# One layer of a hybrid decoder on one core: projecting the values of all heads ahead of the heads

## The reference

```
h = rms_norm(x, norm1_g)                      # x: 1024 tokens x 1024
proj = h @ w_in                               # columns: q 512, k 512, v 512, pool 512, gates 2048
q, k = rms_norm(q), rms_norm(k)               # 4 heads x 2 components x 64
a = (softmax(q1 k1^T / 8) - lam * softmax(q2 k2^T / 8)) v     # causal, v: 128 per head
a = rms_norm(a) * (1 - lam_init)
merged = sigmoid(gate0) * (a @ w_up_attn) + sigmoid(gate1) * (pool_mixer(xp) @ w_up_pool)
x = x + merged @ w_o
x = x + square(relu(rms_norm(x) @ w_mlp_in)) @ w_mlp_out
```

## Time and profile before

| | |
|---|---|
| median of three runs | 1267.37 us (1267.27 to 1267.81) |
| the profiled execution itself | 1267.24 us |
| its span in the profile | 1265.3 us (1.9 us lie around it) |
| PE busy | 98% of the span |
| DVE, ACT, POOL busy | 76%, 44%, 13% |
| granted clock, mean | 1.0 |
| chain that ended last | PE 90%, DVE 5% |

### The profile page before, as it was taken

One profiled execution on the slowest core, in us unless ns is written; L12 is line 12 of the kernel. 1 busy time (PEld: TensorE's weight loads), 2 busy tenths in 40 slices (PEclk: granted clock), 3 DMA queues, 4 the chain that ended last, 5 costly groups with the idle time before them and its releaser, 6 DMA issues.

```text
span 1265.3 us, 17523 instructions
## 1 busy us (share of the span) xinstructions
PE 1241.7 (98%) x6057; PEld 1043.6 (82%) x6057; DVE 960.4 (76%) x1442; ACT 560.9 (44%) x981; POOL 163.8 (13%) x293
## 2 busy tenths in 40 slices
PE   5999999999999999999999999999999999999998
PEld 5888888887888888888887888888888888888887
DVE  5877776768987769774588777777778898879764
ACT  5656555656553323322345455355454433333330
POOL 2433423333100040000000000000000000000034
PEclk9999999999999999999999999999999999999999
DMA  8010010100545466432214544534559644362323
GB/s 264 24 51 18 15 52 1 50 17 17 175 150 191 143 221 215 161 106 93 89 62 141 175 139 144 175 136 148 175 202 355 241 166 167 100 233 100 100 100 133
DMA packets 111816, 165.97 MB, mean 131 GB/s; under 512 B 5357, under 2 KB 59266, under 8 KB 111746
## 3 DMA queue, kind: packets, MB, share of 16 engines
q1 hardware_dynamic: 111746, 165.05, 38.3%
HBM read 116.80 MB, written 48.23 MB: 130 GB/s over the span
## 4 chain that ended last, share of the span: by engine, by line
PE 90%; DVE 5%; issue 2%; ACT 2%; DMA 1%; POOL 0%; SPq 0%; DVEq 0%; ACTq 0%; POOLq 0%
PE bank L2152 83%; PE bank L2331 3%; PE bank L2256 2%; PE bank L2207 1%; DVE c L2061 1%; DVE pair_lo L1955 1%; DMA raw<-in_w_in 1%; PE bank L2461 1%; PE bank L2314 1%; ACT slot_hi L925 0%; DVE wT_lo L1476 0%; DVE slot_lo L1376 0%; DVE small L1469 0%; DVE featT_lo L1391 0%; PE bank L2169 0%
## 5 line engine op out<-in xcount | busy, mean ns | idle before, releaser
L2152 PE MATMUL bank<-o_hi,s_hi 128*128 128x512 f32 x448 | 174.4, 389 | 0.0
L2152 PE MATMUL bank<-o_hi,s_lo 128*128 128x512 f32 x448 | 174.3, 389 | 0.0
L2152 PE MATMUL bank<-slot_hi,featT_hi 128*128 128x384 f32 (+1 forms) x320 | 118.1, 369 | 4.9 <-DVE slot_lo L1376 3.1
L2152 PE MATMUL bank<-slot_lo,featT_hi 128*128 128x384 f32 (+1 forms) x320 | 111.9, 350 | 0.0
L2152 PE MATMUL bank<-slot_hi,featT_lo 128*128 128x384 f32 (+1 forms) x320 | 111.6, 349 | 0.0
L2061 DVE TENSOR_TENSOR c<-bank,c 128x512 f32<-128x512 f32 x112 | 75.7, 689 | 35.0 <-PE bank L2152 33.3
L2152 PE MATMUL bank<-featT_hi,pair_hi 128*128 128x512 f32 x256 | 99.9, 390 | 0.8 <-DVE c L2061 0.6
L2152 PE MATMUL bank<-featT_lo,pair_hi 128*128 128x512 f32 x256 | 99.6, 389 | 0.0
L2152 PE MATMUL bank<-featT_hi,pair_lo 128*128 128x512 f32 x256 | 99.6, 389 | 0.0
L2152 PE MATMUL bank<-o_lo,s_hi 128*128 128x512 f32 x256 | 99.6, 389 | 0.0
L2152 PEld LDWEIGHTS bank<-o_hi,s_hi 128*128 128x128 f32 x448 | 84.1, 188 | 17.7 <-DVE s_lo L2005 0.4
(11 more groups left out here) (250 smaller groups left out, 3159.0 us busy)
## 6 DMA issues: line engine op xcount, KB each, us to landing
s_raw<-u_store SPq DMA_DIRECT2D x28, 1024.0 KB, 5.6
pair_raw<-in_w_mlp_in SPq DMA_DIRECT2D x16, 1024.0 KB, 5.9
u_store<-s_tile SPq DMA_DIRECT2D x64, 256.0 KB, 2.1
o_raw<-in_w_mlp_out SPq DMA_DIRECT2D x16, 1024.0 KB, 7.8
u_store<-u_tile SPq DMA_DIRECT2D x48, 256.0 KB, 2.4
gate_store<-out_tile SPq DMA_DIRECT2D x32, 256.0 KB, 2.1
gate_raw<-in_w_in SPq DMA_DIRECT2D x8, 1024.0 KB, 5.5
raw<-in_w_in SPq DMA_DIRECT2D x15, 512.0 KB, 4.7
```

The lines of the kernel that those rows point to most:

```text
L2152: mm = nc.tensor.matmul(out, a, b, start=start and i == 0, stop=stop and i == len(steps) - 1)
```

## The change

A new stage stands between the start and head 0. SP loads the value columns of w_in for all four heads (load_v_w, four loads of 512 KB with two blocks of features each), ACT and DVE split them into v_w, which lies where qT, kT, v_tok and wT lie later. PE then runs v_project for token tiles 0 to 7, each 24 matmuls of 512 columns into PSUM bank 4 or 5, with x_transpose(t + 1) ahead of v_project(t). ACT and DVE split the result into v_part (two buffers), and SP stores it to DRAM (v_store), 512 KB per tile. The treatment of x is done in this stage; x_transpose and its ACT, DVE and POOL parts leave head 0.

The heads then project q and k only: project is 24 matmuls of 256 columns, qkv is 256 wide, and POOL's split_v is gone. The values of a head are read back to v_tok in one load of 1 MB (load_v): for head 0 after all stores, for heads 1 to 3 when PE has done all products with v of the head before (out_full at T * h). PE waits for it (v_in) ahead of the first product with v of the head. One weight slot less is split between heads. The first exponential waits for all stores of v_part, whose place prob takes.

On ACT the order at the start is now x_square(0), v_w_hi(0), v_w_hi(1), x_hi(0), v_w_hi(2), v_w_hi(3), x_square(1), x_square(2); on DVE x_norm(0), v_w_lo(0), v_w_lo(1), x_lo(0), x_norm(1), v_w_lo(2), v_w_lo(3).

```diff
+        v_w = both("v_w", 96, [P, KD, HEADS * P], 16)
+        v_part = [at(f"v_part{i}", 144 + 4 * i, [P, HEADS, 2, P], F32R) for i in range(2)]
...
-        qkv = [at(f"qkv{i}", kb, [P, 3 * P]) for i, kb in enumerate((156, 157.5, 221))]
+        qkv = [at(f"qkv{i}", kb, [P, 2 * P]) for i, kb in enumerate((156, 157.5, 221))]
...
+        v_store = nc.dram_tensor("v_store", [HEADS, P, T, 2, P], F32, kind="Internal").ap()
...
-            return 2 * b + (t != 1)
+            return 2 * (t % 2) + b
...
+        def v_bank(t):
+
+            return PROJ + t % 2
+
+        def head_w(h, i):
+
+            return HEADS + 3 * h + 1 + i
...
+            def load_x(t):
+
+                wait(sp, h_ready, t - 3)
+                sp.dma_start(x_tile[t % 4][:], x_rows[t]).then_inc(x_in[t % 4], 16)
+
+            def load_v_w(i):
+
+                src = w_in_v[:, 2 * i:2 * i + 2, V0:V0 + HEADS * P]
+                sp.dma_start(k4(raw[i][:], 2), src).then_inc(raw_in[i], 16)
+
+            def load(r, src, left):
+
+                sp.wait_ge(w_ready, left)
+                if not isinstance(left, int):
...
-                dst, n = k4(raw[r][:], parts), parts // pieces
-                for i in range(pieces):
-                    sp.dma_start(dst[:, n * i:n * i + n], src[:, n * i:n * i + n]).then_inc(raw_in[r], 16)
+                sp.dma_start(k4(raw[r][:], KD), src).then_inc(raw_in[r], 16)
...
             def load_head(h):
-                for i, c0 in enumerate((0, K0, V0)):
-                    load(i, w_in_v[:, :, bass.ds(c0 + h * P, P)], 4 * h + 1 + i, pieces=PIECES[i])
-                load(3, w_in_v[:, :, bass.ds(X0 + (GROUPS - 1 - h) * P, P)], 4 * h + 4)
-
-            sp.dma_start(x_tile[0][:], x_rows[0]).then_inc(x_in[0], 16)
-            for i, c0 in enumerate((0, K0, V0)):
-                load(i, w_in_v[:, :, c0:c0 + P], 1 + i, pieces=PIECES[i])
-                if i == 0:
-                    sp.dma_start(g1_row[:], norm1_g.to_broadcast([P, D])).then_inc(g1_in, 16)
-            sp.dma_start(x_tile[1][:], x_rows[1]).then_inc(x_in[1], 16)
-            sp.dma_start(x_tile[2][:], x_rows[2]).then_inc(x_in[2], 16)
+                first = isinstance(h, int)
+                for i, c0 in enumerate((0, K0)):
+                    load(i, w_in_v[:, :, bass.ds(c0 + h * P, P)], 1 + i if first else head_w(h, i) - 3)
+                load(3, w_in_v[:, :, bass.ds(X0 + (GROUPS - 1 - h) * P, P)], 4 if first else head_w(h, 2) - 3)
+
+            def load_v(h):
+
+                if isinstance(h, int):
+                    sp.wait_ge(v_full, T)
+                    sp.wait_ge(v_out, 16 * T)
+                    src = v_store[h:h + 1]
+                else:
+                    sp.wait_ge(out_full, T * h)
+                    apart(sp)
+                    src = v_store[bass.ds(h, 1)]
+                sp.dma_start(v_tok[:].bitcast(F32), src.rearrange("o p t a c -> (o p) t a c")).then_inc(v_in, 16)
+
+            load_x(0)
+            load_v_w(0)
+            sp.dma_start(g1_row[:], norm1_g.to_broadcast([P, D])).then_inc(g1_in, 16)
+            load_v_w(1)
+            load_x(1)
+            load_v_w(2)
+            load_v_w(3)
+            load_x(2)
...
+            def store_v(t):
+
+                sp.wait_ge(v_ready, t + 1)
+                wait(sp, v_out, 16 * t)
+                sp.dma_start(v_store[:, :, t].rearrange("h p a c -> p h a c"), v_part[t % 2][:].bitcast(F32)).then_inc(v_out, 16)
+
+            load_x(3)
+            load_x(4)
+            load_x(5)
+            load_head(0)
+            for t in range(T):
+                if t + 6 < T:
+                    load_x(t + 6)
+                store_v(t)
+            load_v(0)
             with sp.Fori(1, HEADS) as h:
                 load_head(h)
...
 
             def gate_cols(n, width):
                 return w_in_v[:, :, G0 + n * P:G0 + n * P + width]
...
-            def split_v(h, s):
...
-                if not there:
-                    return
-                if t == 0:
-                    wait(pool, out_full, T * of)
-                pool.wait_ge(proj_free, use_of(of, t))
-                apart(pool)
-                v = qkv[t % 3][:, 2 * P:3 * P]
-                pool.tensor_copy(v_tok[:, t, 0, :], v).then_inc(v_hi, 1)
-                pool.wait_ge(v_hi, u + 1)
-                pool.tensor_tensor(v_tok[:, t, 1, :], v, v_tok[:, t, 0, :], ALU.subtract).then_inc(v_ready, 1)
...
-            for t in range(3):
+
+            for t in range(T):
                 x_inverse(t, x_squared, x_mean, x_inv)
...
-                    wait(act, v_ready, u - 1 if t < 2 else u - 2)
-                    nc.scalar.activation(qkv[t % 3][:], bank[:, PROJ, 0:3 * P], ACT.Copy).then_inc(proj_free, 1)
+                    nc.scalar.activation(qkv[t % 3][:], bank[:, PROJ, 0:2 * P], ACT.Copy).then_inc(proj_free, 1)
...
+                if isinstance(u, int) and u == 0:
+                    act.wait_ge(v_out, 16 * T)
...
-                        for i in range(3):
+                        for i in range(2):
                             head_weights(h, i)
...
+            def v_w_hi(i):
+
+                act.wait_ge(raw_in[i], 16)
+                nc.scalar.activation(v_w[0][:, 2 * i:2 * i + 2, :], k4(raw[i][:], 2), ACT.Copy).then_inc(w_hi, 1)
+
+            def v_hi_part(t):
+
+                act.wait_ge(v_full, t + 1)
+                wait(act, v_out, 16 * (t - 1))
+                nc.scalar.activation(v_part[t % 2][:, :, 0, :], k4(bank[:, v_bank(t), :], HEADS), ACT.Copy).then_inc(v_hi, 1)
+
             x_square(0)
-            for i in range(3):
-                split_hi(1 + i, i, PIECES[i], slots[i])
-                if i == 1:
-                    x_hi(0)
+            v_w_hi(0)
+            v_w_hi(1)
+            x_hi(0)
+            v_w_hi(2)
+            v_w_hi(3)
             x_square(1)
             x_square(2)
+            for t in range(T):
+                if t + 1 < T:
+                    x_hi(t + 1)
+                if t + 3 < T:
+                    x_square(t + 3)
+                v_hi_part(t)
+                if t == 4:
+                    act.wait_ge(lam_step, 2)
+                    nc.scalar.activation(lam_exp, lam_sum, ACT.Exp).then_inc(lam_exped, 1)
+                if t == 5:
+                    split_hi(head_w(0, 0), 0, 2, slots[0])
...
-                    if s == 0 and not first:
-                        head_weights(h - 1, 2)
...
+            dve.wait_ge(const_ready, 2)
             for i in range(16):
                 nc.vector.memset(count_inv[:, i:i + 1], 1.0 / (i + 1))
+            def v_w_lo(i):
+
+                dve.wait_ge(w_hi, i + 1)
+                cut = (slice(None), slice(2 * i, 2 * i + 2))
+                nc.vector.tensor_tensor(v_w[1][cut], k4(raw[i][:], 2), v_w[0][cut], ALU.subtract).then_inc(w_ready, 1)
+
+            def v_lo_part(t):
+
+                dve.wait_ge(v_hi, t + 1)
+                part = v_part[t % 2]
+                nc.vector.tensor_tensor(part[:, :, 1, :], k4(bank[:, v_bank(t), :], HEADS), part[:, :, 0, :],
+                                        ALU.subtract).then_inc(v_ready, 1)
+
             x_norm(0)
-            for i in range(3):
-                split_lo(1 + i, i, slots[i])
-                if i == 1:
-                    x_lo(0)
+            v_w_lo(0)
+            v_w_lo(1)
+            x_lo(0)
             x_norm(1)
+            v_w_lo(2)
+            v_w_lo(3)
+            for t in range(T):
+                if t + 1 < T:
+                    x_lo(t + 1)
+                if t + 2 < T:
+                    x_norm(t + 2)
+                v_lo_part(t)
+                if t == 4:
+                    vectors()
+                if t == 5:
+                    split_lo(head_w(0, 0), 0, slots[0])
+                    split_lo(head_w(0, 1), 1, slots[1])
...
                     if t == 0:
-                        pe.wait_ge(w_ready, 4 * h + 3)
-                    if first:
-                        pe.wait_ge(xT_split, 2 * t + 2)
-                    wait(pe, proj_free, use_of(h, t) - 1)
-                out = bank[:, PROJ, 0:3 * P].rearrange("p (m c) -> p m c", m=3)
+                        pe.wait_ge(w_ready, head_w(h, 1))
+                    if isinstance(h, int) and t == 0:
+                        pe.wait_ge(v_ready, T - 1)
+                    else:
+                        wait(pe, proj_free, use_of(h, t) - 1)
+                out = k4(bank[:, PROJ, 0:2 * P], 2)
                 for k in ks:
                     a = cut(featT, ALL, k, slice(t * P, (t + 1) * P))
-                    b = (slot_hi[:, 0:3, k * P:(k + 1) * P], slot_lo[:, 0:3, k * P:(k + 1) * P])
+                    b = (slot_hi[:, 0:2, k * P:(k + 1) * P], slot_lo[:, 0:2, k * P:(k + 1) * P])
...
-                        pe.wait_ge(v_ready, u + 1)
+                        if t == 0:
+                            pe.wait_ge(v_in, 16 * of + 16)
...
+            def v_project(t):
+
+                pe.wait_ge(xT_split, 2 * t + 2)
```

(35 more changed lines are left out.)

71 lines of the change are left out of this document (22 added, 49 removed).

## The result

The changed kernel takes 1288.58 us (median of four, 1288.32 to 1288.65), the kernel before 1267.32 beside it. The ratio is 1.0167, 95% interval 1.015 to 1.0185: slower by 1.7%. The forecast was 1291, its range 1275 to 1303. The profiled execution took 1288.65 us, with a span of 1286.8; before it was 1265.3.

A forecast was written before the change was run, and what follows sets the result against it. The loop's heads were taken as bound by PE and almost as tightly by the chain scores, DVE, ACT, DVE, PE. +39.2 until head 1 and -15.6 in the loop gave +23.6 on 1267.24: 1290.8 us, own range 1284 to 1297, overall 1275 to 1303.

The forecast's parts named there:

- Price of a matmul: PE's matmuls of 256 columns in the heads: 0.121 us each, 0.107 for columns plus 0.014 surcharge; ends 0.107 and 0.175.
- Start: Before the value stage: PE's first projection begins at 20.6 instead of 14.54, 6.1 us later, behind tile 1's square, norm and transposes.
- Value stage: Ahead of head 0: 7.2 us for the first tile, 45.0 for seven more with transposes; ends at 72.8.
- Head 0: First head, starting at 72.8 with an empty pipeline: 47.8 us together, so head 1 starts at 120.6.
- The loop: Heads 1 to 3, summed over steps 0 to 7: 5.2 us less per head, 15.6 for three.
- The values' load: Step 3 of loop heads: the 1 MB load lands in median 5.6 us, 0.5 late; the step counts -0.4.
- POOL's copies: In the heads: 16 copies and subtractions per head cost nothing now; ends for their removal 0 and 0.3 us per head.
- The end: After the loop, from head 4 on: all is as before, no change.
- PE alone sets the pace: Rival, heads: all 31.2 us come back and head 0 is 4 shorter, 1271 us; chance 0.11.
- Load late: Rival, loop heads: value load takes 9.2 instead of 5.6 us, 3.6 more for each of three, 1302; chance 0.10.
- Narrow is no cheaper: Rival, head projections: weight load needs 384 columns' time, loop gives back nothing, head 0 grows some 6 us, 1313; chance 0.05.
- faster: Rival, heads: 256 columns cost 0.107 us and the chain follows PE, 1260 us; chance 0.06.

The follow-up runs named there:

- the other start: Changed kernel with x's tile 1 squared ahead of the last two value weight parts, its transposes in the middle of the first value projection: 1285.32 us.
- the five runs with width, a pass, or the mask changed: Kernel before: 256 columns without values 1249.91, no mask addition 1262.04; changed kernel: 384 columns again 1305.78, two passes of three 1286.88, no mask addition 1280.07 us.
- the load left out: Changed kernel without the 1 MB value loads for heads 1 to 3, which use head 0's values: 1289.95 us.
- the split moved: Pool weights' split moved from step 2 to step 0: changed kernel 1288.78 us, kernel before 1267.85, changed kernel with the other start 1284.57.
- narrowing alone: Kernel before with 256 columns projected in its heads, values not projected, no value stage, stores or value loads: 1249.91 us.
- two passes: Changed kernel with the low-weights pass of the query and key projections left out, 64 matmuls fewer per head: 1286.88 us.
- mask: Causal mask's addition on DVE left out: changed kernel 1280.07 us, kernel before 1262.04 us.
- the load in two: Changed kernel with the other start and the split moved, each value load made in two, tiles 0 and 1 first: 1283.37 us.

## Why the prediction was right

The direction, and 21.3 us against 23.6 forecast. The mechanism is the one forecast: PE gives up 10.3 us per head and idles for half of it, ahead of the transposes of q and k in the five steps that were named (1.54, 1.34, 0.66, 0.43 and 0.69 us in steps 1, 3, 4, 5 and 7), released by DVE. That the sum came within 2.3 us is in part luck: it was too high by 0.8 for the start, by 2.2 for the value stage and by 0.6 for the loop, and too low by the 1.4 us that the end of the kernel lost. Step by step:

- **Price of a matmul, 0.121: held.** A run of 256 columns in the changed kernel starts every 0.120:

```profile
148.75 0.28 PE L2202 MATMUL bank<-slot_hi,featT_hi 128*128 128x256 f32 x1
...
149.71 0.28 PE L2202 MATMUL bank<-slot_lo,featT_hi 128*128 128x256 f32 x1
151.33 0.32 PE L2353 MATMUL bank<-ident,qk_norm 128*128 128x128 f32 x1 [1.34 <-DVE qk_norm L1458]
...
151.55 0.36 PE L2371 MATMUL bank<-v_tok,wT_hi 128*128 128x256 f32 x1
```

- **Start, 6.1 us later: 5.3.** v_project(0) began at 19.82 and not at 20.6. The queue on ACT was as forecast to within 0.3 us (square at 14.67); the eight transposes held PE for 1.6, not 2.0, and the norm of tile 1 ended 0.4 early.
- **Value stage, 52.2 us: 50.0.** Two terms were too big. Some three matmuls ran at the slow pace, not nine, so the first tile took 6.2 and not 7.2. The mistake was to count the slow stretch from the transposes' start with the length that the earlier trace rows showed in the other kernel; the run with the other start had twelve slow ones, up to 19. The time at which it ended was alike in both, 19 to 21, as in the kernel before; how many matmuls fell into it depended on how early PE was fed. The other seven tiles took 43.8, not 45.0: a block of eight transposes cost 0.8 there, not 0.96.
- **Head 0, 47.8: 47.81.** That it fits to a hundredth is luck: steps 0 to 3 took 3.5, 3.6, 4.5 and 5.6, where 3.0, 3.8, 4.3 and 6.0 were forecast.
- **The loop, 5.2 us per head: 5.4.** Steps 0 to 7: 1.9, 0.2, 0.9, 0.1, 0.4, 0.6, 1.4, 0.0, where 1.7, 0.1, 1.3, -0.4, 0.6, 0.5, 1.3, 0.1 were forecast. The argument from the earlier trace rows carried it (the rows show six steps of the eight in which DVE ends within 0.4 us of PE's use or after it, not five as the prediction counted): the five runs with width, a pass, or the mask changed show that the chain binds. Two errors in it cancel. Step 3 was forecast 0.5 late for the values' load, and is not; step 2 gave 0.9 and not 1.3, though no row had shown PE near a wait there.
- **The values' load.** It landed in 4.9 to 5.1 us, not in 5.6, and it lay behind a wait for the norm. The trace of the loads:

```profile
DMA to landing us min/median/max: 4.9/5.0/5.1
```

  The rule of the Trainium skill (DMA: Bandwidth & Descriptors, Anatomy of one DMA, SWDGE path) gave 4.4 as an estimate and "hidden"; it was right on the second, and its time is 0.6 below the measured one. The page fits that rule to DMAs that GpSimd issues; here SP issues them (hardware_dynamic in the page of the profile), so this is no test of it. The rows that I used were of another stage with more traffic beside them. The runs with the load left out and with the split moved show how thin the cover is: it holds against the present step, and no longer once step 3 gets more than 0.1 us shorter.
- **POOL's copies, nothing now and 0 to 0.3 per head as its end: about 0.4.** "PE waits for none of them" was the reason, and it was not enough. PE doesn't wait for them, but it waits for what DVE does, and DVE's norm of q and k took 0.68 us beside them and 0.42 without them, which is most of the 0.36 us between steps 7 and 0 (9.64 and 9.28). The rest of the 0.7 by which the heads of the changed kernel are shorter at the same PE work (65.73 and 65.04) lies mostly where the third weight split stood, for which the prediction had 0.4. This is read from traces, not from a run of its own.
- **The end: 0 forecast, 1.4 measured.** PE waits 1.8 us once for s_lo in the MLP's second half. All kernels that are built on the changed one show such a wait (1.0 to 2.2), and those built on the kernel before at most 0.6. It goes with the longest landing among the 28 loads of s_raw. That was 14.4 to 15.0 us in the kernel before and those built on it, in the others it went from 15.4 (PE waits 1.0) over 15.7 (1.3) and 16.2 (1.8) to 16.6 (2.2). Why that load lands later stays open, and no run tried it.

The rivals: "PE alone sets the pace" is refuted by three runs (narrowing alone, two passes, mask). "Load late" was refuted: the load landed in 4.9 to 5.1 us and not in 9.2. With the split moved PE does wait for it, because the norm comes earlier and not because the load comes later. "Narrow is no cheaper" and "faster" fell with the pace of 0.120.

## What to carry to other kernels

PE at 98% does not say that PE's work is the bound: look, step by step, at how long before PE's next item the engines that feed it had finished. If that is tenths of a microsecond, work taken from PE is worth only those steps in which nothing else stands that near, here half of it, while the same work added in another stage costs its full price. And a wait that is removed shows the next one: before moving work off a chain, find out what else lands at that moment.

## What the runs showed of the hardware

PE's granted clock fell when PE had waited inside a head, and stayed low for some time after it was busy again. In the kernel with the other start it happened in step 1 of head 1, after a wait of 1.54 us (windows of 1 us):

```profile
132.00:133.00 1.00, 0.07 (x1) 0.00 (x0) 1.00 (x2) 1.00 (x3) 0.00 (x0) 1.00 0.00 0
133.00:134.00 1.00, 0.38 (x3) 0.39 (x4) 1.00 (x3) 1.00 (x2) 0.00 (x0) 1.00 0.00 0
134.00:135.00 1.00, 1.00 (x11) 1.00 (x10) 0.90 (x5) 0.89 (x5) 0.00 (x0) 0.99 0.00 0
135.00:136.00 1.00, 1.00 (x7) 1.00 (x7) 1.00 (x2) 0.44 (x3) 0.00 (x0) 0.50 0.00 0
```

It stayed at 0.50, which is 1.2 GHz, until about 138.4, and the head took 66.3 in place of 65.0. The same wait of 1.54 us stands in the same step of the changed kernel, whose clock stayed at 1.00. So a wait of that length doesn't always do it. The same happened in step 1 of one head in the kernel narrowed alone (behind a wait of 1.60 us) and in the one with the load in two (1.69), and in no other head of the loop in either. With 4.6 us it did in each of three heads, for some 6 us, and with a third of the projections' matmuls gone, where the wait in step 1 is 2.49, in each of four. A gap on PE can thus cost more than its own length: 1.1 to 1.3 us beyond a gap of 1.5 to 1.7, 1.8 beyond one of 4.6. It also makes small gains hard to measure, since the runs of one kernel then differ by 2 to 3 us (1282.05 to 1285.51), where those of the kernel before beside them differ by 1.4.

In the kernel narrowed alone and in the one before, DVE's norm of q and k takes 0.68 us in step 0, beside POOL's subtraction of the values, and 0.42 where POOL has none. POOL's copy and subtraction take 0.98 and 1.32 us beside DVE's weight splits, 0.29 and 0.46 elsewhere. No run was made for this alone.
